# Two PSUM banks in turn for the small products of a state-space stage, in a two-layer hybrid backbone step

## What is computed

```python
def ssd_chunked(x, dt, A, B, C, init_state):
    ...
    acum = jnp.moveaxis(jnp.cumsum(dtc * A.reshape(G, HG), axis=2), 2, -1)
    cb = jnp.einsum('bcign,bcjgn->bcgij', Cc, Bc)
    w_intra = cb[:, :, :, None] * jnp.exp(seg)
    y_diag = jnp.einsum('bcghij,bcjghp->bcighp', w_intra, dtx)
    decay_to_end = jnp.exp(acum[..., -1:] - acum)
    chunk_states = jnp.einsum('bcghj,bcjgn,bcjghp->bcghpn', decay_to_end, Bc, dtx)
    ...
    y_off = jnp.einsum('bcign,bcghpn,bcghi->bcighp', Cc, S_in, jnp.exp(acum))
    y = (y_diag + y_off).reshape(b, L, SSD_HEADS, P)
    return y, S_final.reshape(b, SSD_HEADS, P, N)
```

## Time and profile before

| | |
|---|---|
| runs | 1439.53, 1440.29, 1440.70 us, median 1440.29 |
| the profiled execution | 1437.26 us, of which the profiled span 1435.5 |
| instructions in the profile | 20909 |
| PE matmul busy | 1407.6 us, 98% |
| PE weight load busy | 1304.4 us, 91% |
| DVE, ACT, POOL busy | 915.8 (64%), 672.5 (47%), 113.9 (8%) us |
| chain that ended last | PE 91%, DMA 3%, DVE 3%, ACT 1% |
| DMA | 222.97 MB, mean 155 GB/s |
| mean granted clock of PE | 0.997 of full |

### The profile page before, as it was taken

One profiled execution on the slowest core, in us unless ns is written; L12 is line 12 of the kernel. 1 busy time (PEld: TensorE's weight loads), 2 busy tenths in 40 slices (PEclk: granted clock), 3 DMA queues, 4 the chain that ended last, 5 costly groups with the idle time before them and its releaser, 6 DMA issues.

```text
span 1435.5 us, 20909 instructions
## 1 busy us (share of the span) xinstructions
PE 1407.6 (98%) x8209; PEld 1304.4 (91%) x8209; DVE 915.8 (64%) x1515; ACT 672.5 (47%) x1252; POOL 113.9 (8%) x102
## 2 busy tenths in 40 slices
PE   6999999899999999999999999999999999999998
PEld 3988888788899998999989998889989999999998
DVE  6677564675566676767666876667746675555562
ACT  4746545343635425252536565553435453434252
POOL 0000102320001000000010011041300010000000
PEclk9999999999999999999999999999999999999999
DMA  9665427575346667755336442355443434343431
GB/s 362 189 220 172 128 74 235 183 227 154 110 131 211 219 235 241 256 162 159 121 80 189 123 111 67 102 161 162 147 132 105 131 118 129 121 127 123 126 125 44
DMA packets 191193, 222.97 MB, mean 155 GB/s; under 512 B 11263, under 2 KB 156791, under 8 KB 191095
## 3 DMA queue, kind: packets, MB, share of 16 engines
q1 hardware_dynamic: 191094, 221.64, 48.8%
HBM read 217.58 MB, written 4.03 MB: 154 GB/s over the span
## 4 chain that ended last, share of the span: by engine, by line
PE 91%; DMA 3%; DVE 3%; ACT 1%; issue 1%; SPq 0%; POOL 0%; ACTq 0%; DVEq 0%
PE bank L778 24%; PE bank L779 24%; PE bank L780 24%; PE bank L798 2%; PE bank L799 2%; PE bank L800 2%; PE bank L822 1%; PE seg_ps L986 1%; PE y_ps L1075 1%; PE y_ps L1012 1%; PE y_ps L1106 1%; DMA back_rows<-acs_rows 1%; PE y_ps L1002 1%; DMA dts<-in_w_mod_dram 1%; DMA ahead_rows<-acs_rows 1%
## 5 line engine op out<-in xcount | busy, mean ns | idle before, releaser
L1690 DVE TENSOR_TENSOR wlo<-raw,whi 128x1024 fp32r<-128x1024 f32 (+1 forms) x288 | 351.8, 1229 | 208.7 <-ACT whi L1242 207.0
L778 PE MATMUL bank<-ahi,whi 128*128 128x384 f32 (+1 forms) x1280 | 443.3, 346 | 0.9 <-DVE wlo L1690 0.9
L1242 ACT CAST whi<-raw 128x1024 fp32r<-128x1024 f32 (+1 forms) x288 | 296.0, 1035 | 303.9 <-PE bank L780 207.5
L780 PE MATMUL bank<-ahi,wlo 128*128 128x384 f32 (+1 forms) x1280 | 432.9, 338 | 0.0
L779 PE MATMUL bank<-alo,whi 128*128 128x384 f32 (+1 forms) x1280 | 432.8, 338 | 0.0
L778 PE MATMUL bank<-bhi,whi 128*128 128x384 f32 x768 | 264.2, 344 | 0.5 <-DVE tb L1982 0.5
L779 PE MATMUL bank<-blo,whi 128*128 128x384 f32 x768 | 259.4, 338 | 0.0
L780 PE MATMUL bank<-bhi,wlo 128*128 128x384 f32 x768 | 259.3, 338 | 0.0
L778 PEld LDWEIGHTS bank<-ahi,whi 128*128 128x128 f32 x1280 | 241.3, 189 | 11.3 <-issue 8.3
L779 PEld LDWEIGHTS bank<-alo,whi 128*128 128x128 f32 x1280 | 241.4, 189 | 3.5 <-issue 2.9
L780 PEld LDWEIGHTS bank<-ahi,wlo 128*128 128x128 f32 x1280 | 241.1, 188 | 0.0
(11 more groups left out here) (280 smaller groups left out, 1431.4 us busy)
## 6 DMA issues: line engine op xcount, KB each, us to landing
raw<-in_w_mlp_dram SPq DMA_DIRECT2D x128, 512.0 KB, 3.6
raw<-in_w_in_dram SPq DMA_DIRECT2D x104, 512.0 KB, 4.0
raw<-in_w_mod_dram SPq DMA_DIRECT2D x64, 512.0 KB, 5.9
raw<-in_w_ssd_o_dram SPq DMA_DIRECT2D x16, 512.0 KB, 3.5
raw<-in_w_out_dram SPq DMA_DIRECT2D x16, 512.0 KB, 3.5
arena_g<-in_w_mod_dram SPq DMA_DIRECT2D x13, 512.0 KB, 4.5
arena_s<-in_w_mod_dram SPq DMA_DIRECT2D x12, 512.0 KB, 6.5
ahead_rows<-acs_rows SPq DMA_DIRECT2D x12, 512.0 KB, 5.3
```

The costliest lines, as they stand in the source:

```text
L778: nc.tensor.matmul(dst, uh[:, k, tm_cols(m)], hi[k0 + k], start=first and k == 0, stop=False)
L780: ins = nc.tensor.matmul(dst, ul[:, k, tm_cols(m)], hi[k0 + k], start=False, stop=last and k == 3)
L1242: nc.scalar.copy(dst, src).then_inc(hi_ready, 1)
L1690: nc.vector.tensor_tensor(rest, full, top.bitcast(F32), ALU.subtract).then_inc(lo_ready, 1)
```

## The change

Products n alternate between `aux` and `seg_ps[:, 0]`, counted through both groups of a layer (`spot`), and the diagonal products between `ybank` and `seg_ps[:, 1]` (`y_spot`). The semaphore `aux_free` is gone. In its place each kind of reader has a semaphore of its own, raised by the operation that reads the bank: `products_taken`, `st_ready`, `state_moved`, `state_staged`, `y_taken`. `single` waits for the reader of the product two before (`spot_freed`). ACT no longer waits for its own copies. A diagonal product waits for the `y_diag` two before. `yoff` gets a wait for the state that it reads, which the count of `aux_free` had implied. The order of instructions on every engine is as before, and so is their number.

```diff
             return slice(i * P, (i + 1) * P)
+
+        def spot(g, n):
+
+            return (aux, seg_ps[:, 0, :])[(g * 11 + n) % 2]
+
+        def spot_freed(l, g, n):
+
+            b = l * 2 + g
+            if n == 0:
+                return products_taken, b + 1
+            if n <= 2:
+                return st_ready, b * 2 + n
+            if n <= 4:
+                return state_moved, b * 2 + n - 2
+            if n <= 6:
+                return state_staged, b * 2 + n - 4
+            return y_taken, b * 4 + n - 6
+
+        def y_spot(g, t):
+
+            return (ybank, seg_ps[:, 1, :])[(g * TT + t) % 2]
 
...
-                    if n or g:
-                        pe.wait_ge(aux_free, (l * 2 + g) * 11 + n)
+                    before = g * 11 + n - 2
+                    if before >= 0:
+                        signal, value = spot_freed(l, before // 11, before % 11)
+                        pe.wait_ge(signal, value)
+                    return spot(g, n)
...
-                    if t or g:
-                        pe.wait_ge(y_free, (l * 2 + g) * 3 + t)
+                    if g * TT + t >= 2:
+                        pe.wait_ge(y_free, (l * 2 + g) * 3 + t - 1)
                     for h in range(HG):
-                        ins = nc.tensor.matmul(ybank[:, h * 64:h * 64 + 64], ew[:, (g + t) % 2, h, :],
+                        ins = nc.tensor.matmul(y_spot(g, t)[:, h * 64:h * 64 + 64], ew[:, (g + t) % 2, h, :],
...
-                        single(g, n)
+                        dst = single(g, n)
                         a, b = CV[t]
-                        nc.tensor.matmul(aux, bc_cm[:, 2 + g, a:b], st[:, s, :], start=True, stop=True).then_inc(aux_done, 1)
+                        if s < 2:
+                            pe.wait_ge(st_ready, (l * 2 + g) * 2 + 2)
+                        else:
+                            pe.wait_ge(state_moved, (l * 2 + g) * 2 + (2 if s == 2 else 1))
+                        nc.tensor.matmul(dst, bc_cm[:, 2 + g, a:b], st[:, s, :], start=True, stop=True).then_inc(aux_done, 1)
 
...
-                    def keep(n, dst, signal, value):
-                        evac(g, n, dst, signal)
-                        act.wait_ge(signal, value)
-                        act.sem_inc(aux_free, 1)
+                    def keep(n, dst, signal):
+
+                        act.wait_ge(aux_done, (l * 2 + g) * 11 + n + 1)
+                        nc.scalar.copy(dst, spot(g, n)).then_inc(signal, 1)
...
-                    nc.vector.tensor_tensor(st[:, dst, :], st[:, dst, :], aux, ALU.add).then_inc(aux_free, 1)
+                    nc.vector.tensor_tensor(st[:, dst, :], st[:, dst, :], spot(g, n), ALU.add).then_inc(state_moved, 1)
...
-                    nc.vector.tensor_tensor(xbuf[:, t, cols], dtx[:, (g + t) % 2, :], ybank, ALU.add).then_inc(y_free, 1)
+                    nc.vector.tensor_tensor(xbuf[:, t, cols], dtx[:, (g + t) % 2, :], y_spot(g, t), ALU.add).then_inc(y_free, 1)
...
-                    nc.vector.tensor_tensor(heads(ytmp), heads(aux), per_head(eac, t, e, g), ALU.mult).then_inc(aux_free, 1)
-                    dve.wait_ge(aux_free, (l * 2 + g) * 11 + n + 1)
+                    nc.vector.tensor_tensor(heads(ytmp), heads(spot(g, n)), per_head(eac, t, e, g), ALU.mult).then_inc(y_taken, 1)
+                    dve.wait_ge(y_taken, (l * 2 + g) * 4 + n - 6)
```

More of the change, by code:

```diff
@@ L1081, in state_sum @@
                     def state_sum(n, t):
-                        single(g, n)
+                        dst = single(g, n)
                         pe.wait_ge(dtxd_ready, (l * 2 + g) * 4 + n - 2)
-                        nc.tensor.matmul(aux, b_tm[:, t, tm_cols(g)], dtxd[:, n - 3, :], start=True, stop=True).then_inc(aux_done, 1)
+                        nc.tensor.matmul(dst, b_tm[:, t, tm_cols(g)], dtxd[:, n - 3, :], start=True, stop=True).then_inc(aux_done, 1)
                     def end_state(n, e):
-                        single(g, n)
+                        dst = single(g, n)
                         pe.wait_ge(dtxd_ready, (l * 2 + g) * 4 + 3 + e)
                         for j in range(4):
-                            ins = nc.tensor.matmul(aux[:, tm_cols(j)], dtxd[:, e, tm_cols(j)], b_tm[:, 0, tm_cols(g)], start=True,
+                            ins = nc.tensor.matmul(dst[:, tm_cols(j)], dtxd[:, e, tm_cols(j)], b_tm[:, 0, tm_cols(g)], start=True,
                                                    stop=True, skip_group_check=True)
@@ L1096, in transposes4 @@
                     def transposes4(n, src):
-                        single(g, n)
+                        dst = single(g, n)
                         for j in range(4):
-                            ins = nc.tensor.transpose(aux[:, tm_cols(j)], src[:, tm_cols(j)], ident)
+                            ins = nc.tensor.transpose(dst[:, tm_cols(j)], src[:, tm_cols(j)], ident)
                         ins.then_inc(aux_done, 1)
                     def yoff(n, t, e, s):
-                        single(g, n)
+                        dst = single(g, n)
                         a, b = CV[t]
-                        nc.tensor.matmul(aux, bc_cm[:, 2 + g, a:b], st[:, s, :], start=True, stop=True).then_inc(aux_done, 1)
+                        if s < 2:
[3 more added lines that the diff above has]
+                        nc.tensor.matmul(dst, bc_cm[:, 2 + g, a:b], st[:, s, :], start=True, stop=True).then_inc(aux_done, 1)
                     def inner_products():
-                        single(g, 0)
+                        dst = single(g, 0)
                         for t, (a, b) in enumerate(CV):
-                            ins = nc.tensor.matmul(aux[:, tm_cols(t)], bc_cm[:, g, a:b], bc_cm[:, 2 + g, a:b], start=True, stop=True,
+                            ins = nc.tensor.matmul(dst[:, tm_cols(t)], bc_cm[:, g, a:b], bc_cm[:, 2 + g, a:b], start=True, stop=True,
                                                    skip_group_check=True)
@@ L1153, in _ @@
                     if l == 0 and i == 3:
-                        pe.wait_ge(aux_free, 22)
+                        pe.wait_ge(y_taken, 8)
                         mod_columns(0, 1)
@@ L1158, in _ @@
                 pe.wait_ge(yn_ready, l * TT + TT)
-                pe.wait_ge(aux_free, (l + 1) * 22)
+                pe.wait_ge(y_taken, (l + 1) * 8)
                 pe.wait_ge(modc_ready, l * 2 + 2)
@@ L1553, in _ @@
                     row_sum(g, 0)
-                    keep(1, st[:, 0, :], st_ready, (l * 2 + g) * 2 + 1)
+                    keep(1, st[:, 0, :], st_ready)
                     fill(slot[1])
-                    keep(2, st[:, 1, :], st_ready, (l * 2 + g) * 2 + 2)
+                    keep(2, st[:, 1, :], st_ready)
                     decay_exp(g, 0)
@@ L1563, in _ @@
                     row_sum(g, 2)
-                    keep(5, stage[:, 1, :], state_staged, (l * 2 + g) * 2 + 1)
-                    keep(6, stage[:, 2, :], state_staged, (l * 2 + g) * 2 + 2)
+                    keep(5, stage[:, 1, :], state_staged)
+                    keep(6, stage[:, 2, :], state_staged)
                     decay_exp(g, 2)
@@ L2096, in take_products @@
                             dve.wait_ge(w_ready, (l * 2 + g) * 3)
-                        nc.vector.tensor_copy(cbs[:], aux[:, 0:T].rearrange("p (t n) -> p t n", t=TT)).then_inc(aux_free, 1)
-                        dve.wait_ge(aux_free, (l * 2 + g) * 11 + 1)
+                        nc.vector.tensor_copy(cbs[:], spot(g, 0)[:, 0:T].rearrange("p (t n) -> p t n", t=TT)).then_inc(products_taken, 1)
+                        dve.wait_ge(products_taken, l * 2 + g + 1)
                     slot = SSD_SLOTS[g]
```

7 lines of the change are left out of this document (2 added, 5 removed).

## The result

The changed kernel takes 1432.11 us, median of six executions (1429.53 to 1433.65), against 1439.79 for the kernel before beside it (six executions, 1435.64 to 1440.70): ratio 0.9947, 95% interval 0.9931 to 0.9962, so 7.7 us faster (5.5 to 9.9). The profiled execution takes 1431.99 us with a span of 1430.2, against 1437.26 and 1435.5: 5.3 us between the two profiled executions and 7.7 between the medians. That gap of 2.4 us is the first thing to explain.

What follows compares the result with a forecast made beforehand. PE, busy 98% of the span, bounds the kernel; only its idle or low-clock time can be won. 1.44 + 1.10 + 0.60 + 0.60 = 3.74 us off the 1440.29 median gives 1436.6 us, range 1434.7 to 1439.6.

Steps and rivals of the forecast that it cites:

- the four places: State-space stage, groups 0 and 1 of layers 0 and 1: where PE's waits for bank releases were priced.
- Group 1: `end_state(6)` follows the diagonal product directly, since PE waits only for the bank: 1.44 us in layer 0, 1.10 in layer 1.
- Group 0, the bank's own part: Diagonal product t=1 starts 0.60 us earlier in each layer; the idle moves behind `end_state(5)` and ends with `weigh`.
- DVE itself does not get earlier: Group 0: DVE's unbroken chain from `pick` ends at the same time, so removing the transposes' 0.7 us wait gains 0.
- The clock in layer 0: Group 0's fall to 1.2 GHz stays; 0.60 us gain taken, between bounds of 0.30 and 2.0.
- rival A: Layer 0, group 0: the low clock ends earlier, 1.4 us more gain, 5.1 in all, 1435.2 us; chance 0.22.
- rival B: Layer 1, group 0: a new clock fall behind 2.4 us idle loses some 3.1 us; gain 0.6, 1439.7 us; chance 0.16.
- I take the same 3.7 us off: The gain computed on the profiled execution is subtracted unchanged from the median of the runs, 1440.29 us.
- The waits added at `yoff` and removed on ACT: Second semaphore wait on 16 `yoff` products, upper bound 12.8 us, and ACT's dropped waits for itself: both costed at 0.

Runs made afterwards that it cites:

- the filled pair: Old and changed kernel, each with discarded products filling TensorE's waits in group 0 of both layers: 1433.76 and 1428.70 us.
- e1: The changed kernel measured again, nothing altered: 1430.96 us, ratio 0.9945 to the kernel before.
- e2: Changed kernel with the diagonal products back on one bank, only the products n alternating: 1434.01 us, ratio 0.9957 to the kernel before.
- e8: Changed kernel with ACT's removed waits for its own copies put back: 1431.99 us, ratio 0.9947 to the kernel before.
- e4: Changed kernel with the first transposes' wait for the copy of the inner products put back in group 0 of both layers: 1433.04 us.
- e3: Changed kernel with the products n back on one bank, only the diagonal products alternating: 1437.85 us, ratio 0.9986 to the kernel before.
- e5: Kernel before, with discarded products (three in layer 0, one in layer 1) ahead of group 0's `end_state(5)`: 1433.76 us, ratio 0.9959.
- e7: Changed kernel with DVE's `weigh` of the second tile put ahead of `next_state(4)`: 1426.62 us, ratio 0.9910 to the kernel before.
- e9: Changed kernel with `weigh` moved between the two merges of the filler on DVE: 1423.96 us, ratio 0.9899 to the kernel before.

## Why the prediction was wrong, point by point

The direction was right, and so was what PE waits for in the four places. The size was not: 3.7 us forecast, 7.7 measured. By the filled pair 5.1 of them are waits and 2.6 the clock. Two steps failed: that DVE does not get earlier, and that the falls of one execution are those of all.

- **Group 1** (1.44 and 1.10): measured 1.45 and 1.10. The bank was all that PE waited for, and the distance from start to start gave the size.
- **Group 0, the bank's own part** (0.60 each). From `weigh`'s start to the diagonal product it was 1.96 us in both layers (260.92 - 258.96, 970.97 - 969.01) and is 1.27 now (259.13 - 257.86, and the same in layer 1): 0.69 each, nearly the forecast. The idle did move behind `end_state(5)` in one piece, 3.06 us for the 3.1 forecast in layer 0, 2.20 for 2.4 in layer 1.
- **"DVE itself does not get earlier" (0).** This step failed. Counted from the inner products, `weigh` starts 0.55 us earlier in layer 0 and 0.44 in layer 1 than before. In layer 1 the removed wait at the transposes lets SP issue the back rows' DMA 0.89 us earlier, since it stands behind a weight load that waits for PE; the forecast had looked at DVE's unbroken chain and not at what starts it. In layer 0 no such wait was there; the DMA took 6.94 us from issue to POOL instead of 7.50, and 6.3 to 7.8 in the other kernels, so this part is scatter. In layer 1 it is the change: over all traces `weigh` ends 0.66 us earlier without the wait than with it.
- **The sum of these** in the two profiled executions: 1.45 + 1.10 + 0.69 + 0.69 + 0.55 + 0.44 = 4.9 us, beside 5.1 by the filled pair. With layer 0's scatter at nothing and layer 1 at the 0.66 of all traces it is 4.6, where the forecast had 3.7.
- **The clock in layer 0** (the fall kept, 0.60 taken between 0.30 and 2.0). The low stretch was halved, as in rival A, whose own price of 1.4 us came out as 1.34. But that is luck of the execution: it was about 3.4 us in e1 and e2 too, and in e8 and e4, behind idle pieces of 3.06 and 3.07 us as in the profiled execution above, 6.8 us as in the old kernel. Two stretches of e8:

```profile
259.25:262.65 3.40, 2.83 (x13) 2.83 (x14) 3.33 (x5) 0.00 (x0) 2.08 (x1) 0.52 0.00 0
262.65:266.05 3.40, 3.40 (x20) 1.25 (x20) 3.26 (x5) 0.00 (x0) 0.00 (x0) 0.50 0.00 0
```

- **The clock in layer 1** (rival B). The fall came, behind 2.20 us of idle, and cost 1.62 us in the profiled execution. A and B held at once, and nearly cancel there. In e1 and e8 the fall of layer 1 did not come.
- **"I take the same 3.7 us off", for the median.** This is the step that failed most. It took the profiled execution's falls for those of all executions. The old kernel was already 3.0 us slower in the median than in that execution; that was a sign of falls which the one trace did not show. The profile of e3, with the old waits at the products n, shows such a fall in layer 1 (clock 0.72 and 0.59), where the old kernel's had 1.00:

```profile
968.00:973.00 5.00, 4.43 (x25) 4.26 (x26) 4.90 (x7) 0.59 (x1) 2.08 (x1) 0.72 0.19 56
973.00:978.00 5.00, 5.00 (x22) 5.00 (x22) 2.99 (x4) 2.46 (x3) 0.00 (x0) 0.59 0.17 52
```

```profile
968.00:973.00 5.00, 3.18 (x26) 3.02 (x27) 4.90 (x7) 0.59 (x1) 2.08 (x1) 1.00 0.18 52
973.00:978.00 5.00, 5.00 (x33) 5.00 (x33) 3.54 (x5) 1.88 (x3) 0.00 (x0) 1.00 0.23 61
```

  What belongs into the sum is the loss that falls cost on the mean, not the loss in one trace: filling the waits of group 0 measured it at 5.9 us for the old kernel and 3.3 for the new.
- **The waits added at `yoff` and removed on ACT** (0 and 0): right; no wait stands at L1135, and e8 shows ACT's.
- **What the chances missed.** A and a small B were in the range as alternatives, each worked from one execution. No case had the old kernel losing more than its trace showed.
- **The Trainium skill**, "TensorE: Matmul & The Clock Gate", section on HAM oscillation, has a kernel where PSUM double-buffering "gave no further gain". Here it gave 0.5%, since the bank's release alone ended the waits in group 1. The same page's section "A second HAM failure mode: psum-queue depth-cycling" describes short idle pieces that let the clock swing between its levels; the traces agree with it in three of the four places of this stage (falls behind both waits of group 0, and behind the one of group 1 in layer 0 in e5), and where the two of group 0 were filled the profiled executions show none.

What stays open: how the 7.7 us divide more closely than 3.3 to 5.3 of waits and the rest of clock, and why the clock fell behind waits of 1.07 us (e7, layer 1) and 1.25 (e4, layer 1) and not behind 1.73 (e7, layer 0) and 1.75 (e1, layer 1).

## What to carry to other kernels

When PE's waits are short and its clock falls behind some of them, one profiled execution does not price them: compare its time and granted clock with those of the other executions first, and price a wait with the fall that may follow it. Discarded products in the wait are a cheap way to measure that price. And when a resource is freed, reorder what had been written around it: the same exchange on DVE cost 2 us with one bank and gave 5 with two, and the best place of `weigh` gave 7 to 8.

## What had not been expected of the hardware

- Executions of one kernel on one chip differ in the falls of the clock: mean granted clocks from 0.991 to 0.997 in 45 executions of the old kernel (the three sets, each on one chip), whose times spread from 1435.3 to 1443.9 us. A straight line through the 17 of the first set gives 1.1 us for each 0.001 of the clock.
- Work that nobody needs made a kernel faster: four discarded 128x512 fp32 products took 5.9 us off the old kernel.
- The length of a wait did not decide whether the clock fell behind it (1.07 us with a fall, 1.75 without), nor for how long it stayed low (3.4 or 6.8 us behind the same 3.06).
- A DVE operation that runs while GpSimd starts its 128x1024 sum (L2340, 2.2 us) took about 1.6 us longer in these traces, whichever it was: the 128x512 product 2.27 us instead of 0.68 in the changed kernel, the 128x1024 product 2.80 instead of 1.22 in e7; in e9 the 1.6 us spread over two (1.95 for 1.22, 1.67 for 0.82).
